# The inverse of the delta rule: its transpose made on VectorE by 32x32 blocks, instead of by products on TensorE

## What is computed

```python
L = jnp.where(strict, jnp.einsum('bnhid,bnhjd->bnhij', k_beta, k) * decay, 0.0)
eye = jnp.eye(C, dtype=q.dtype)
rhs = jnp.concatenate([v_beta, k_beta * jnp.exp(G)[..., None]], axis=-1)
sol = lax.linalg.triangular_solve(eye + L, rhs, left_side=True, lower=True)
u, w = sol[..., :dv], sol[..., dv:]
```

## Time and profile before

| | |
|---|---|
| median of 3 runs | 1128.18 us (1127.96 to 1128.94) |
| profiled execution, its own time | 1130.11 us |
| its span, first to last instruction | 1128.3 us |
| TensorE busy | 1121.9 us (99%), 10319 matmul instructions |
| VectorE busy | 749.5 us (66%) |
| ScalarE busy | 589.0 us (52%) |
| GpSimd busy | 165.5 us (15%) |
| granted TensorE clock, mean | 1.000 |
| HBM | 189.76 MB read, 169 GB/s over the span |

### The profile page before, as it was taken

One profiled execution on the slowest core, in us unless ns is written; L12 is line 12 of the kernel. 1 busy time (PEld: TensorE's weight loads), 2 busy tenths in 40 slices (PEclk: granted clock), 3 DMA queues, 4 the chain that ended last, 5 costly groups with the idle time before them and its releaser, 6 DMA issues.

```text
span 1128.3 us, 23303 instructions
## 1 busy us (share of the span) xinstructions
PE 1121.9 (99%) x10319; PEld 1102.1 (98%) x10319; DVE 749.5 (66%) x853; ACT 589.0 (52%) x698; POOL 165.5 (15%) x108
## 2 busy tenths in 40 slices
PE   9999999999999999999999999999999999999998
PEld 7999999999999999999999999999899999999998
DVE  7888755353566997796779767655576566756453
ACT  7776442423855765564766434424797346434341
POOL 0002532000141100000366200000010012201000
PEclk9999999999999999999999999999999999999999
DMA  8445423243465555555555544345444555555552
GB/s 310 142 153 176 151 87 111 76 150 113 150 225 187 187 187 189 193 202 201 160 210 186 176 165 147 125 160 171 172 137 171 192 200 202 183 196 187 189 194 103
DMA packets 27603, 192.29 MB, mean 170 GB/s; under 512 B 3056, under 2 KB 3184, under 8 KB 4848
## 3 DMA queue, kind: packets, MB, share of 16 engines
q1 hardware_dynamic: 27504, 190.82, 49.4%
HBM read 189.76 MB, written 1.05 MB: 169 GB/s over the span
## 4 chain that ended last, share of the span: by engine, by line
PE 97%; ACT 1%; DMA 1%; DVE 1%; POOL 0%; issue 0%; DVEq 0%
PE psS L615 60%; PE psP L615 17%; PE psS L603 7%; PE psS L541 2%; PE psP L938 1%; PE psP L791 1%; PE psP L780 1%; PE psP L912 1%; PE psP L889 1%; PE psP L795 1%; PE psP L670 1%; PE psP L842 1%; PE psP L851 0%; POOL ss L1783 0%; DMA raw<-in_wts 0%; PE psP L631 0%
## 5 line engine op out<-in xcount | busy, mean ns | idle before, releaser
L1349 DVE TENSOR_TENSOR wl<-raw,wh 128x2048 fp32r<-128x2048 f32 (+1 forms) x178 | 419.5, 2359 | 117.4 <-ACT wh L986 116.3
L986 ACT ACTIVATE wh<-raw 128x2048 fp32r<-128x2048 f32 x176 | 337.0, 1915 | 250.9 <-DMA raw<-in_wts 250.2
L615 PE MATMUL psS<-Yh,wh 128*128 128x256 f32 x1040 | 295.9, 285 | 0.3 <-DVE Yl L1355 0.3
L615 PE MATMUL psS<-Yl,wh 128*128 128x256 f32 x1040 | 288.6, 278 | 0.0
L615 PE MATMUL psS<-Yh,wl 128*128 128x256 f32 x1040 | 288.6, 278 | 0.0
L615 PE MATMUL psS<-Xh,wh 128*128 128x256 f32 x848 | 240.0, 283 | 0.3 <-PE psS L615 0.3
L615 PE MATMUL psS<-Xl,wh 128*128 128x256 f32 x848 | 235.8, 278 | 0.0
L615 PE MATMUL psS<-Xh,wl 128*128 128x256 f32 x848 | 235.8, 278 | 0.0
L615 PEld LDWEIGHTS psS<-Yh,wh 128*128 128x128 f32 x1040 | 196.1, 189 | 3.1 <-issue 1.9
L615 PEld LDWEIGHTS psS<-Yl,wh 128*128 128x128 f32 x1040 | 195.8, 188 | 2.5 <-issue 1.9
L615 PEld LDWEIGHTS psS<-Yh,wl 128*128 128x128 f32 x1040 | 195.3, 188 | 0.0
(11 more groups left out here) (270 smaller groups left out, 1956.4 us busy)
## 6 DMA issues: line engine op xcount, KB each, us to landing
raw<-in_wts SPq DMA_DIRECT2D x176, 1024.0 KB, 4.8
raw<-in_wts SPq DMA_DIRECT2D x2, 512.0 KB, 6.0
gdn<-in_x SPq DMA_DIRECT2D x1, 1024.0 KB, 7.4
out<-head SPq DMA_DIRECT2D x4, 256.0 KB, 2.1
head<-in_x SPq DMA_DIRECT2D x1, 516.0 KB, 4.0
head<-in_x SPq DMA_DIRECT2D x1, 512.0 KB, 6.0
xf<-in_dr SPq DMA_DIRECT2D x1, 512.0 KB, 5.6
xf<-in_md SPq DMA_DIRECT2D x1, 384.0 KB, 6.1
```

The lines of the kernel that those rows point to most:

```text
L615: mm = pe.matmul(bank[:, half], a[:, n % SLOTS, p, :], b[:, kk_, :], start=(first and i == 0), stop=(last and i == 2), skip_group_check=True)
L986: act.activation(wh[:, n % SLOTS], raw[:, n % SLOTS], ACT.Copy).then_inc(sem["wh"], 1)
L1349: return dve.tensor_tensor(out, a, b, op)
```

## The change

TensorE loses the step `lev0t` and the transposed product in `right`. VectorE makes `TI` by its transpose instruction, which transposes each 32x32 block where it stands: once for each half in a step `lev0t` of its own, placed first among the steps of turn 18, and at levels 0 to 3 behind the subtraction from `SI`. As `TI` is used at levels 0 to 4, where `SI` has diagonal blocks of 2 to 32 and zeros elsewhere, transposing by 32x32 blocks gives the whole transpose. ScalarE loses its step `lev0t`, and `psP1` is no longer used here. `left(0, p)` waits for `vb` 4 as well; `right` waits for `st` up to the subtraction of the piece before, not its transpose; what `lev0t` waited for (`eg`, `lt`) moves into `right(0, p)`.

```diff
@@ schedule()
     put(17, "lev0")
-    put(18, "lev0t")
+    todo[18].insert(0, ("lev0t", ()))
     for l in range(5):
         put(19 + l, "level", l)
@@ TensorE
-            def lev0t():
-                pe.wait_ge(sem["eg"], 8)
-                pe.wait_ge(sem["lt"], 24)
-                for p in range(2):
-                    pe.wait_ge(sem["s0"], 2 * p + 2)
-                    crossed(p, lambda c, b, q: pe.matmul(
-                        halves(p)[ROWS[c], b, q], eight(SIc, p)[ROWS[c], b, q], ident[ROWS[c], ROWS[c]],
-                        start=True, stop=True, skip_group_check=True)).then_inc(sem["t0"], 1)
-
             def left(l, p):
                 i = 2 * l + p
                 pe.wait_ge(sem["bs"], i + 1)
                 if l == 0:
                     pe.wait_ge(sem["t0c"], p + 1)
                     pe.wait_ge(sem["tok"], 8)
+                    pe.wait_ge(sem["vb"], 4)
                 else:
                     pe.wait_ge(sem["st"], 2 * (i - 2) + 2)
...
                 pe.wait_ge(sem["pc"], i + 1)
                 if l == 0:
-                    pe.wait_ge(sem["t0c"], 2)
+                    pe.wait_ge(sem["eg"], 8)
+                    pe.wait_ge(sem["lt"], 24)
                 if i:
-                    pe.wait_ge(sem["st"], 2 * i if i <= 8 else 17)
-                mm = crossed(p, lambda c, b, q: pe.matmul(
+                    pe.wait_ge(sem["st"], 2 * i - 1)
+                crossed(p, lambda c, b, q: pe.matmul(
                     halves(0)[ROWS[c], b, q], packed(ss[p])[ROWS[c], b, q], eight(SIc, p)[ROWS[c], b, q],
-                    start=True, stop=True, skip_group_check=True))
-                if l < 4:
-                    mm = crossed(p, lambda c, b, q: pe.matmul(
-                        halves(1)[ROWS[c], b, q], eight(SIc, p)[ROWS[c], b, q], packed(ss[p])[ROWS[c], b, q],
-                        start=True, stop=True, skip_group_check=True))
-                mm.then_inc(sem["pb_"], 1)
+                    start=True, stop=True, skip_group_check=True)).then_inc(sem["pb_"], 1)
@@ ScalarE
-            def lev0t():
-                for p in range(2):
-                    act.wait_ge(sem["t0"], p + 1)
-                    act.activation(eight(TIc, p), halves(p), ACT.Copy).then_inc(sem["t0c"], 1)
@@ VectorE
+            def flat8(t, p):
+
+                return t[:, 4 * p:4 * p + 4].rearrange("p h t m -> p (h t) m")
+
+            def lev0t():
+                for p in range(2):
+                    dve.wait_ge(sem["s0"], 2 * p + 2)
+                    dve.transpose(flat8(TIc, p), flat8(SIc, p)).then_inc(sem["t0c"], 1)
+
             def update(l, p):
-                dve.wait_ge(sem["pb_"], 2 * l + p + 1)
-                for q, dst in enumerate((SIc, TIc)[:2 if l < 4 else 1]):
-                    v = eight(dst, p)
-                    tt(v, v, halves(q), ALU.subtract, "st")
+                i = 2 * l + p
+                dve.wait_ge(sem["pb_"], i + 1)
+                v = eight(SIc, p)
+                tt(v, v, halves(0), ALU.subtract, "st")
+                if l < 4:
+                    dve.wait_ge(sem["st"], 2 * i + 1)
+                    dve.transpose(flat8(TIc, p), flat8(SIc, p)).then_inc(sem["st"], 1)
```

More of the change, by code:

```diff
@@ L284 @@
 og ogh on onr or orh out pa_ par pb_ pc pe pn pt qd qk r1 r2 r3 raw0 raw1 raw2 raw3 rawh rb rd res4 rg ri rl ro row rr rs rsp rt rtT
-rtk rtp ry s0 sc sg silu sp sq sqh sqp sqr sr ss ss0 ssa st t0 t0c tap tb tk tok tsa uw uwp vb nrw nrh nr r2c rb2 rh vn warm wh wh0 wl wl0 xq ws x0 x0h
+rtk rtp ry s0 sc sg silu sp sq sqh sqp sqr sr ss ss0 ssa st t0c tap tb tk tok tsa uw uwp vb nrw nrh nr r2c rb2 rh vn warm wh wh0 wl wl0 xq ws x0 x0h
 x1 x1h x2 x3 x3h xT xTb xb xbh xres ya yah zp zs
@@ L952, in _ @@
             steps = {"norm": norm, "ab_mm": ab_mm, "ab_tok": ab_tok, "ab_cum": ab_cum, "hsq": hsq, "qrow": qrow, "onorm": onorm,
-                     "rmsh": rmsh, "rows": rows, "kk": kk, "tok": tok, "lev0t": lev0t, "level": level, "lastlevel": lastlevel, "uw": uw,
+                     "rmsh": rmsh, "rows": rows, "kk": kk, "tok": tok, "level": level, "lastlevel": lastlevel, "uw": uw,
                      "state": state, "wstate": wstate, "o": o, "rtok": rtok_, "att_s": att_s_, "att_t": att_t,
@@ L1316, in _ @@
                      "pieces": pieces, "qhi": qhi, "ab_ts": ab_ts,
-                     "rows": rows, "mixc": mixc, "tok": tok, "lev0t": lev0t, "level": level, "uw": uw, "state": state, "o": o,
+                     "rows": rows, "mixc": mixc, "tok": tok, "level": level, "uw": uw, "state": state, "o": o,
                      "onorm": onorm, "mix": mix, "res1": res1, "res2": res2, "sum2": sum2,
@@ L1739, in _ @@
                      "zg": zg, "gate1": gate1, "ab_mm": ab_mm, "ab_tok": ab_tok, "ab_den": ab_den, "ab_decay": ab_decay, "ab_cum": ab_cum,
-                     "qsum": qsum, "qhi": qhi, "kk": kk, "tok": tok, "level": level, "lastlevel": lastlevel, "state": state, "wstate": wstate,
+                     "qsum": qsum, "qhi": qhi, "kk": kk, "tok": tok, "lev0t": lev0t, "level": level, "lastlevel": lastlevel, "state": state, "wstate": wstate,
                      "onorm": onorm, "mixc": mixc, "mix": mix, "res1": res1, "res2": res2, "sum2": sum2, "res3": res3, "x2": x2,
```

## The result

The changed kernel takes **1118.02 us** (median of 4 runs, 1117.51 to 1119.36), beside it the kernel before 1128.11 us (4 runs, 1127.96 to 1128.94): ratio 0.9909, 95% interval 0.9897 to 0.992. Faster, by 10.1 us where the prediction had 9.0. Two later comparisons gave 0.9908 and 0.9913. The profiled execution took 1118.39 us.

What follows compares the result with a forecast made beforehand. TensorE was taken to bound the kernel: 9.65 us of its work removed, less a 0.65 us wait, gives 9.0 us saved and a median of 1119.2 us. Range 1118.0 to 1121.9 us.

Steps and rivals of the forecast that it cites:

- What bounds the kernel: Whole kernel: TensorE, busy 1121.9 of 1128.3 us; work given to VectorE is free unless TensorE waits for it.
- (a): TensorE in the levels: removing the transposed twin product L795, 8 pieces of 0.93 us, saves 7.4 us.
- (b): TensorE before the levels: removing `lev0t`, 2.01 us, and its way back to weight products, 0.20 us, saves 2.2 us.
- A transpose at 0.65 us: VectorE: each of ten 128x512 f32 transposes takes 0.65 us, from the nearest row, a subtraction of 0.68 us.
- The wait, 0.65 us: At `left(0,0)`: TensorE waits once, 0.65 us, for `tok(3)`'s products, which VectorE does behind the two first transposes.
- Rival 1: At `left(0,0)`: no wait at all, so all 9.65 us stay saved, 1118.5 us; chance 0.11.
- rival 2: VectorE's transpose goes through its data twice, 1.3 us; wait 1.95 us at `left(0,0)`, 1120.5 us; chance 0.13.
- rival 3: VectorE becomes the bound of the levels, transposes of 3.6 us each: slower, 1134.5 us; chance 0.02.
- The levels hidden: In the levels: subtraction, transpose and hand-over, 1.45 us, fit in TensorE's 3.04 us before `left(l+1,1)`; no wait there.
- VectorE's sum up by 1 us: VectorE's busy time: 8 subtractions go and 10 transposes come, +1 us, hidden beside TensorE in the levels.
- the period of 10.06 us: In the levels: one level's period on TensorE falls from 11.93 to 10.06 us, with no TensorE wait.
- Rival 4: TensorE's clock falls in the new wait and the weight products behind it slow down; given no chance of its own.

Runs made afterwards that it cites:

- before: The kernel without the change, the base of the comparisons: median 1128.11 us beside the changed kernel.
- after: The changed kernel, compared with the kernel without the change: median 1118.02 us, ratio 0.9909.
- the 1.5 us run: The changed kernel with one more transpose ahead of `tok(3)`, lengthening the wait at `left(0,0)`: 1118.81 us, ratio 0.9914 against the kernel without the change.

## Why the prediction was right or wrong

- **What bounds the kernel**: right. TensorE kept 96% of the chain, and VectorE's new work ended one wait in the whole program.
- **(a), the twin product, 7.4 us**: right, 7.47 measured alone.
- **(b), `lev0t` and its way back, 2.2 us**: right. With the transposes a turn earlier, no wait and the slow pace, the stretch is 9.68 us shorter, where (a) and (b) make 9.65. The kernel without the drain at 36 shows 9.65 less 0.72 to within 0.05 us.
- **A transpose at 0.65 us**: 0.71 by itself, 0.61 from start to start in a pair. By the estimate from the Trainium skill's table ("VectorE: DVE Perf Modes", section "The three transpose paths"), 1.24 us, the time would have been 1120.4; the trace disagrees with it. The nearest row, the subtraction over the same pattern, was the better guide.
- **The wait, 0.65 us**: 0.7 measured, by errors that nearly cancel: the pair took 1.22 us and not 1.30, `tok(3)`'s products 1.24 and not 1.28, the hand-over 147.14 - 146.88 = 0.26 us and not 0.1. Rival 1 (no wait) and rival 2 (1.95 us) fall, and so does rival 3: 0.71 us is far from 3.6, and nothing waits in the levels.
- **The levels hidden**: right, with room; even doubled transposes caused no wait there. In the fullest level VectorE went straight from the split to the subtraction (155.87 + 2.29 = 158.16, then 158.23), just as `right(0,1)` ended at 158.18: "just free", as forecast.
- **VectorE's sum up by 1 us**: it went up by 0.1. The transposes add 7.0 us and 4.8 us of subtractions go, but the splits came out shorter (414.9 us in all against 417.0). Nothing hung on it.
- **The step that failed: the period of 10.06 us, with "a weight product costs 0.117 us"** taken for a constant. It is one of two paces. Behind the 0.7 us wait that the change brings, the level stretch ran at the other in three of four executions, 0.16 us a level and 0.9 us in all. So the wait that was put down as a loss of 0.65 us came out at nothing. The stretch was 8.88 us shorter at the slow pace (71.78 us, without the drain at 36) and 9.81 at the quick one; the other 0.3 of the 10.1 us is within the interval of the ratio, 9.0 to 11.6 us. A sign of it stood in the first numbers: before's profiled execution took 1.93 us more than the median, which the prediction carried along as a constant. It fits the 2.7 us of blocks 36 to 49.
- **The range's lower end, 1118.0 us**: the result stands on it, at 1118.02. It allowed 0.5 us for scatter, from 0.98 us between three runs. The executions of before in all comparisons lie between 1127.69 and 1131.12 us.
- **Rival 1's number, 1118.5 us, is near the result for another reason**: the wait is there, and given back. The kernel with the wait removed is no faster than after.
- **Rival 4** had no chance of its own. At 0.7 and 1.5 us it does not happen; at 2.2 us it does, for 1.4 us. Whether it would have behind rival 2's 1.95 us, no run shows; if so, rival 2 would have come out near 1121.9 us and not at 1120.5. The range had room for it, the arithmetic did not.

## What to carry to other kernels

Where one engine is the bound to 99%, count its instructions, then read the spacing of its most frequent one in several executions before taking it as a price: half a percent of the kernel may hang on it, and a removed wait may pay nothing. Judge a change by the stretch it touches as well as by the whole, since untouched stretches moved by 2.7 us between executions of one program. Before work is moved to another engine, ask first how long its result makes the bound engine stand still: 0.7 us was free here, 2.2 us cost 3.8 (74.77 us of stretch against 80.66 - 9.65 = 71.01).

## What the hardware showed that was not expected

- **Two paces at one clock.** Weight products start every 0.113 or 0.118 us, with the granted clock at 1.00 in both, and can keep either for hundreds of products. The Trainium skill, "TensorE: Matmul & The Clock Gate", section "Wait — 56ns, not 53.3ns?", gives N/2.4 GHz plus about 2.5 ns for matmuls back to back, an estimate of 109 ns for these 256 columns. Neither pace is that; here each product also loads weights of its own (PE and PEld both have 9999 instructions), so the cases differ.
- **What turns it is only partly known.** A wait of 0.7 to 1.5 us did in six executions of seven, shorter ones at that place in none of eight. The edit that adds the wait alone shows that nothing need be removed for it. But the execution that kept the slow pace had the same wait, to 0.01 us, and the same program so far, and in block 40 of the 1.5 us run the quick pace was lost at an irregularity of 0.1 us. The drain at 36 gave 77.3 us for blocks 36 to 49 in six profiles, about 80.0 in seven and 79.22 in one, with the same code there. What decides in those cases, and what in TensorE or in its operands' supply the two paces are, stays open. Most edits here have one profile each; a longer series of one kernel, which would give the odds of each pace, was not tried.
- **A clock that falls in mid-program.** Behind 2.2 us of waiting it stood at 0.50 for a little over 3 us in three executions of four, by their mean clocks.
